# Sampled attention: masks laid into the score buffer, one operation that adds and takes the maximum, and two side products in other places

## What is computed

```python
def sel_attend(q, idx, q_pos, blocks, slopes):
    ...
    kv = blocks[b_ix, g_ix, idx]
    s = jnp.einsum('btgrd,bngjd->btgrnj', q, kv[..., 0, :])
    k_pos = idx[..., None] * SEL_BLOCK + jnp.arange(SEL_BLOCK, dtype=jnp.int32)
    dist = q_pos[None, :, None, None, None] - k_pos
    s = s - slopes[None, None, :, :, None, None] * dist[:, :, :, None].astype(jnp.float32)
    ...
    p = jax.nn.softmax(s.reshape(s.shape[:4] + (-1,)), axis=-1).reshape(s.shape)
    ...
    return jnp.einsum('btgrnj,btgnjd->btgrd', p, kv[..., 1, :])
```

## Time and profile before

| | |
|---|---|
| time, median of 3 runs | 2636.42 µs (2633.18 to 2641.44) |
| profiled execution: its time, its span | 2633.0 µs, 2630.7 µs |
| TensorE products busy | 2474.3 µs, 94% of the span |
| TensorE weight loads busy | 1994.0 µs, 76% |
| VectorE busy | 794.6 µs, 30% |
| ScalarE busy | 525.1 µs, 20% |
| GpSimd busy | 97.0 µs, 4% |
| mean granted TensorE clock | 0.957 of full speed |
| chain that ended last | PE 87%, DVE 7%, DMA 2%, ACT 2%, issue 1% |

### The profile page before, as it was taken

How to read it: one execution, slowest core, us unless ns; L and a number is a source line. 1 busy time by engine, 2 the same in 40 slices (tenths; PEclk the granted TensorE clock), 3 DMA queues, 4 the chain that set the end, 5 groups by cost and what they waited for, 6 DMA issues and landing times.

```text
span 2630.7 us, 31111 instructions
## 1 busy us (share of the span) xinstructions
PE 2474.3 (94%) x13222; PEld 1994.0 (76%) x13222; DVE 794.6 (30%) x1829; ACT 525.1 (20%) x1067; POOL 97.0 (4%) x182
## 2 busy tenths in 40 slices
PE   7999789999998999999999987999999989999998
PEld 5787567678887888888877865766788878888886
DVE  2444333642412112210015543356431122112001
ACT  1254111550101111110012531135310011111100
POOL 3010000000000000000000100000000000000000
PEclk8998899997999999999999978999989999999999
DMA  6444421111221222222262534211112212221222
GB/s 194 126 170 176 186 71 49 33 33 35 64 83 48 64 80 64 81 57 67 73 209 91 202 144 177 65 49 25 27 48 80 67 48 80 64 81 59 64 72 67
DMA packets 184576, 228.52 MB, mean 87 GB/s; under 512 B 37470, under 2 KB 170932, under 8 KB 180084
## 3 DMA queue, kind: packets, MB, share of 16 engines
q1 hardware_dynamic: 174008, 133.11, 17.2%
q0 software_dynamic: 10432, 93.44, 9.4%
HBM read 218.19 MB, written 16.66 MB: 89 GB/s over the span
## 4 chain that ended last, share of the span: by engine, by line
PE 87%; DVE 7%; DMA 2%; ACT 2%; issue 1%; DVEq 0%; SPq 0%; POOLq 0%; ACTq 0%
PE PS L790 50%; PE PS L1336 12%; PE PS L812 5%; PE PS L909 4%; DVE arena L1650 3%; PE PS L897 2%; ACT arena L1367 2%; PE PS L1141 1%; DMA arena<-in_cache_kv_slc_dram,idx 1%; PE PS L1152 1%; PE PS L1057 1%; PE PS L433 1%; DVE arena L1641 1%; PE PS L1254 1%; DMA arena<-in_state_kv_win_dram 1%
## 5 line engine op out<-in xcount | busy, mean ns | idle before, releaser
L790 PE MATMUL PS<-hT,ring 128*128 128x272 f32 x4608 | 1081.0, 397 | 14.0 <-DVE hT L1647 10.7
L790 PEld LDWEIGHTS PS<-hT,ring 128*128 128x128 f32 x4608 | 882.4, 192 | 208.6 <-issue 25.9
L1367 ACT ACTIVATE arena<-PS 64x512 f32<-64x512 f32 (+10 forms) x480 | 241.9, 525 | 1295.3 <-PE PS L790 709.7
L1336 PE MATMUL PS<-arena,ring 128*128 128x272 f32 x1408 | 323.5, 393 | 1.9 <-DVEq L2225 1.9
L1336 PEld LDWEIGHTS PS<-arena,ring 128*128 128x128 f32 x1408 | 267.2, 190 | 57.6 <-DVEq L2225 2.7
L1650 DVE COPY arena<-PS 64x512 f32<-64x512 f32 (+6 forms) x215 | 155.8, 726 | 323.3 <-PE PS L790 103.1
L1641 DVE TENSOR_TENSOR arena<-PS,arena 128x544 f32<-128x544 f32 (+3 forms) x120 | 73.1, 621 | 418.9 <-PE PS L790 399.5
L790 PE MATMUL PS<-arena,ring 128*128 128x272 f32 x768 | 177.2, 393 | 3.1 <-DVE arena L1641 3.1
L1647 DVE SCALAR_TENSOR_TENSOR arena<-arena,prm 128x32 f32<-128x32 f32 (+1 forms) x176 | 87.9, 500 | 291.2 <-ACT arena L1367 288.1
L790 PEld LDWEIGHTS PS<-arena,ring 128*128 128x128 f32 x768 | 145.8, 190 | 33.9 <-DVE arena L1641 4.0
L1641 DVE TENSOR_TENSOR xT<-PS,xT 128x544 f32<-128x544 f32 x32 | 23.2, 724 | 427.0 <-PE PS L1336 319.1
(11 more groups left out here) (278 smaller groups left out, 1644.9 us busy)
## 6 DMA issues: line engine op xcount, KB each, us to landing
ring<-in_w_up_dram SPq DMA_DIRECT2D x88, 512.0 KB, 4.6
ring<-in_w_in_dram SPq DMA_DIRECT2D x68, 512.0 KB, 4.7
ring<-in_w_down_dram SPq DMA_DIRECT2D x32, 384.0 KB, 3.8
ring<-in_w_down_dram SPq DMA_DIRECT2D x32, 320.0 KB, 4.4
arena<-in_state_kv_win_dram POOLq DMA_DIRECT2D x4, 2048.0 KB, 15.7
ring<-in_w_out_dram SPq DMA_DIRECT2D x16, 512.0 KB, 4.5
out_dram<-in_state_kv_win_dram POOLq DMA_DIRECT2D x2, 4064.0 KB, 22.7
ring<-in_w_in_dram SPq DMA_DIRECT2D x16, 256.0 KB, 4.8
```

The source lines that it names most:

```text
L790: mm = pe.matmul(PS[0:m, b + a, 0:HALF], weight(k), rhs(k)[:, HALF * a:HALF * a + HALF], start=(k == 0), stop=(k == nk - 1))
L1336: mm = pe.matmul(PS[:, b + a, 0:HALF], w[:, k, :], aT[:, 11 * half + k, HALF * a:HALF * a + HALF], start=(half == 0 and k == 0), stop=(hal ...
L1367: return nc.scalar.activation(out, in_, func, **kw)
```

## The change

Four things change.

1. The masks are laid into `z` before the scores come. Behind `window_values(hf)`, VectorE adds the chosen blocks' mask and the distances over all 2048 columns, copies the new tokens' scores and takes their maximum. When the scores of two quarters are there, one operation (`tensor_tensor_reduce`) adds them to what lies in `z` and takes the maximum of the sum. The window does likewise with `dwin`. The maxima of the parts are joined by small operations.
2. The window's steps of the first half are split: `window_probabilities(0)` (the transposes) comes ahead of the importance product, and `window_values(0)` behind the transposes of the compressed probabilities. A buffer `ptnw` of its own takes the window's new-token probabilities.
3. The side products move: `qb0` from behind the first window's scores to behind the compressed branch's output product, ahead of `turn_k(0)`; `kb1` from behind the second half's gathered scores to behind `window_values(1)`, ahead of `turn_k(0)` of that half. The places ("s", hf, 2) are new there, and ("s", 1, 0) is empty.
4. The value product of the gathered keys waits for the probabilities' two copies one by one, the first ahead of block 0, the second ahead of block 8, and for `ptn` at the end.

The diff, cut to its core:

```diff
-at = dict(zip((("s", 0, 2), ("s", 0, 0), ("s", 1, 1), ("s", 1, 0)), SIDE))
+at = dict(zip((("s", 0, 2), ("s", 0, 0), ("s", 1, 1), ("s", 1, 2)), SIDE))
...
-def window_values(hf):
...
-    xw = XB[xslot(f"win{hf}")[0]].rearrange("p l c -> p (l c)").rearrange("p (b r c) -> p b r c", b=4, r=4)
...
+def window_probabilities(hf):
...
+def window_values(hf):
...
+    xw = XB[xslot(f"win{hf}")[0]].rearrange("p l c -> p (l c)").rearrange("p (b r c) -> p b r c", b=4, r=4)
...
         bb = 32 * b4
-        mm = pe.matmul(PS[bb:bb + 32, b, 0:P], ptn[0:NS, bb:bb + 32], kv[0:NS, 4, 2, P:2 * P], start=False, stop=True)
+        mm = pe.matmul(PS[bb:bb + 32, b, 0:P], ptnw[0:NS, bb:bb + 32], kv[0:NS, 4, 2, P:2 * P], start=False, stop=True)
     mm.then_inc(*S.fill(pe, f"ow{hf}"))
...
 window_scores(0)
-side(("s", 0, 2))
+window_probabilities(0)
 pe.wait_ge(*S.at(pe, "pc_s", 1))
...
 mm.then_inc(*S.fill(pe, "pcT"))
+window_values(0)
 pe.wait_ge(*S.drained(pe, "pcT"))
...
         window_scores(hf)
-    window_values(hf)
+        window_probabilities(hf)
+        window_values(hf)
+    side(("s", hf, 2))
...
     b = S.banks(pe, f"os{hf}")
-    pe.wait_ge(*S.drained(pe, f"pt{hf}0"))
-    pe.wait_ge(*S.drained(pe, f"pt{hf}1"))
-    pe.wait_ge(*S.drained(pe, f"ptn{hf}"))
     for i in range(STRIDE):
+        if i % 8 == 0:
+            pe.wait_ge(*S.drained(pe, f"pt{hf}{i // 8}"))
         for b4 in range(4):
...
                       start=(i == 0), stop=False)
+    pe.wait_ge(*S.drained(pe, f"ptn{hf}"))
     for b4 in range(4):
...
+dv.wait_ge(*S.drained(dv, "sn"))
...
+    copy(zw[:, 512:512 + NS], snew[:, 2 + hf, :])
+    rmax(small[:, 100:101], snew[:, 2 + hf, :])
...
-    tt(zw[:, 0:512], PS[:, b, :], dwin[:, :], ALU.add).then_inc(*S.drain(dv, f"sw{hf}"))
+    nc.vector.tensor_tensor_reduce(zw[:, 0:512], PS[:, b, :], dwin[:, :], 1.0, -3e38, ALU.add, ALU.max, small[:, 99:100]).then_inc(*S.drain(dv, f"sw{hf}"))
...
-    copy(zw[:, 512:512 + NS], snew[:, 2 + hf, :]).then_inc(*S.inc(dv, "dve_step"))
-    dv.wait_ge(*S.last(dv, "dve_step"))
-    rmax(small[:, 23:24], zw).then_inc(*S.inc(dv, "dve_step"))
-    dv.wait_ge(*S.last(dv, "dve_step"))
-    tsc(small[:, 34:35], small[:, 23:24], nslope_c, ALU.mult).then_inc(*S.inc(dv, "nb_s"))
+    tsc(small[:, 34:35], small[:, 99:100], small[:, 100:101], ALU.max, nslope_c, ALU.mult).then_inc(*S.inc(dv, "nb_s"))
...
-side_copy(("s", 0, 2))
...
     dv.wait_ge(*S.last(dv, "dve_step"))
+    z4 = z[:, 0:2048].rearrange("p (l s f) -> p l s f", l=STRIDE, f=4)
+    tt(z4, bc(selml[:, :, :].unsqueeze(3), [P, STRIDE, NSEL - 1, 4]),
+       bc(dslc[:, :].rearrange("p (s f) -> p s f", f=4).unsqueeze(1), [P, STRIDE, NSEL - 1, 4]), ALU.add).then_inc(*S.inc(dv, "dve_step"))
+    copy(z[:, 2048:2048 + NS], snew[:, hf, :])
+    rmax(small[:, 98:99], snew[:, hf, :]).then_inc(*S.inc(dv, "dve_step"))
+    side_copy(("s", hf, 2))
+    dv.wait_ge(*S.last(dv, "dve_step"))
     turned_keys(dv, copy, hf, 0, 1)
...
-        tt(z[:, 1024 * lg:1024 * lg + 1024].rearrange("p (m n) -> p m n", m=8), PS[:, b:b + 2, :].rearrange("p a (m n) -> p (a m) n", m=4),
-           bc(dslc[:, :].unsqueeze(1), [P, 8, P]), ALU.add).then_inc(*S.drain(dv, f"ss{hf}{lg}"))
-    dv.wait_ge(*S.drained(dv, f"ss{hf}0"))
-    dv.wait_ge(*S.drained(dv, f"ss{hf}1"))
-    copy(z[:, 2048:2048 + NS], snew[:, hf, :])
-    z4 = z[:, 0:2048].rearrange("p (l s f) -> p l s f", l=STRIDE, f=4)
-    tt(z4, z4, bc(selml[:, :, :].unsqueeze(3), [P, STRIDE, NSEL - 1, 4]), ALU.add).then_inc(*S.inc(dv, "dve_step"))
-    dv.wait_ge(*S.last(dv, "dve_step"))
-    rmax(small[:, 22:23], z[:, :]).then_inc(*S.inc(dv, "dve_step"))
-    dv.wait_ge(*S.last(dv, "dve_step"))
-    tsc(small[:, 32:33], small[:, 22:23], nslope_c, ALU.mult).then_inc(*S.inc(dv, "nb_s"))
+        zl = z[:, 1024 * lg:1024 * lg + 1024]
+        nc.vector.tensor_tensor_reduce(zl, PS[:, b:b + 2, :].rearrange("p a n -> p (a n)"), zl, 1.0, -3e38, ALU.add, ALU.max,
+                                       small[:, 96 + lg:97 + lg]).then_inc(*S.drain(dv, f"ss{hf}{lg}"))
+        dv.wait_ge(*S.drained(dv, f"ss{hf}{lg}"))
+        if lg == 0:
+            tt(small[:, 98:99], small[:, 98:99], small[:, 96:97], ALU.max).then_inc(*S.inc(dv, "dve_step"))
+            dv.wait_ge(*S.last(dv, "dve_step"))
+    tsc(small[:, 32:33], small[:, 97:98], small[:, 98:99], ALU.max, nslope_c, ALU.mult).then_inc(*S.inc(dv, "nb_s"))
```

7 lines of the change are left out of this document (4 added, 3 removed).

## The result

| | before | changed |
|---|---|---|
| median, range of the runs | 2638.39 µs (2633.18 to 2641.44, 4 runs) | 2596.56 µs (2592.55 to 2599.19, 4 runs) |
| profiled execution: time, span | 2633.0, 2630.7 µs | 2598.69, 2596.8 µs |
| mean granted TensorE clock | 0.957 | 0.963 |

The changed kernel takes 0.9842 of the time before, 95% interval 0.9819 to 0.9865: 41.8 µs less. The forecast was 2607, in a range of 2598 to 2620. The direction held, but the median lies 1.4 µs under the range, and the gain is half again as large as the 27.8 µs forecast. A second set of four runs had its median at 2598.60, just inside the range.

What follows compares the result with a forecast made beforehand. TensorE was taken as busy nearly throughout, losing time only to waits and low clock. Per layer 7.8 + 1.1 + 1.8 + 1.0 + 4.7 = 16.4, less 2.5, is 13.9, 27.8 for two: 2607 µs, range 2598 to 2620.

Steps and rivals of the forecast that it cites:

- first half, up to the scores: Samples' first half: gather issued earlier, side product covers its wait, gathered scores begin at 270.6 instead of 278.43; 7.8 µs per layer.
- first half, after the scores: Behind the first half's gathered scores: side product stays, shorter VectorE path removes the 1.14 µs wait; 1.1 µs per layer.
- first value product: First half's value product of gathered keys: waits only for its first eight blocks at its start; 0.9 µs per layer.
- second half, up to the scores: Second half: side product fills the gathers' waits, but full DMA engines limit the gain; 1.0 µs per layer.
- second half, after the scores: Behind the second half's last scores: uncovered wait of 3.9 µs, ending at 349.8 instead of 354.55; 4.7 µs per layer won.
- second value product and the clock: Second half: 0.9 µs won by the value product's split wait, 2.5 lost to low clock behind the new wait, per layer.
- the side product, begun at the low clock, takes 8.8: First half, side product ahead of turning the gathered keys: starts at low clock, takes 8.8 µs as before, ends at 266.4.
- second rival: First half: clock rises earlier, small operations win back 1.6 µs, side product 1.2, capped at some 2 per layer; 2603, chance 0.12.
- 1.0 won, nothing if the weight load ... delays the last slice: Second half's gathers: 1.0 µs per layer won, none if the side product's released weight load delays the last slice a µs.
- I take 2.5: Behind the second half's new wait: low clock costs 2.5 µs per layer, between bounds of nothing and 7.8.
- first rival: Behind the new wait the clock stays low to the next side product: 7.8 instead of 2.5 µs per layer; 2618, chance 0.14.
- fourth rival: Slower: low clock holds far into the prompt's part, costing 29.2 µs per layer; 2659, chance 0.03.

Runs made afterwards that it cites:

- window_steps_late: The changed kernel with the first half's window transposes and values back behind the compressed branch's output product; 2608.15 µs, ratio 0.9879.
- kb1_old_place: The changed kernel with side product `kb1` back behind the second half's gathered scores; 2604.12 µs, ratio 0.9871.
- before_waits_filled: The kernel before with dummy transposes of the constant identity in TensorE's uncovered waits in the sampled stretch; 2631.44 µs, ratio 0.9973.

## Why the prediction was right in kind and too low in size

Per layer, in the traces of the forecast's kernel and of the changed one, µs won:

| term | forecast | layer 0 | layer 1 |
|---|---|---|---|
| first half, up to the scores | 7.8 | 9.00 | 9.95 |
| first half, after the scores | 1.1 | 1.36 | 1.59 |
| first value product | 0.9 | 1.12 | 1.12 |
| second half, up to the scores | 1.0 | −0.45 | 0.45 |
| second half, after the scores | 4.7 | 4.74 | 4.75 |
| second value product and the clock | 0.9 − 2.5 | −1.83 | −0.20 |
| sum | 13.9 | 13.9 | 17.7 |

The sum of layer 0 meets the forecast to the tenth by luck: the first half won 1.7 more than forecast, the second half's way to its scores 1.5 less, and the last row 0.2 less. The 3.8 above the forecast lie in layer 1.

**What held.** Each step that was to show is in the trace: no wait for a slice in the first half and 0.80 in the second of layer 0; the fourth gather of the first half issued 8.3 after the window's scores end; the combined operation at 1.2; one wait of 3.90 where 3.9 was forecast; the clock at 0.56 behind it. The transposes of the window start 4.02 after its scores began (forecast 4.05), and the side product 6.34 after that (forecast 6.5).

**First failed step: "the side product, begun at the low clock, takes 8.8".** It took 7.70 in layer 0 and 7.60 in layer 1. With the split, TensorE works through the small operations without a gap (6.14 of 7 µs busy at 0.50), and the clock is back as the product starts. In layer 1 it came back earlier still, and the small operations took 5.36 instead of 6.5 as well. window_steps_late, which has the waits again, gives the 8.89 of the forecast. So the second rival, given 0.12, came true for about half of its 2 µs in layer 0 (and in full in the second trace of the changed kernel, 21.4 instead of 22.4) and all of it in layer 1. The sum had counted the gap-free run as three waits removed and nothing more; what it does to the clock stood only in that rival.

**Second: "1.0 won, nothing if the weight load ... delays the last slice".** In layer 0 0.45 were lost. The side product took 9.66, not 8.8 or 9.05, but that is not what decided: a shorter one would only have made the 0.80 behind it longer. The last slice did. By the trace's DMA records the window and the four slices, 10 MB on GpSimd's queue, took 29.2 µs (291.6 to 320.8), where they had taken 28.1 (305.3 to 333.4); and from the wait's end to the scores it took 3.1 instead of the 2.7 counted. The forecast had said that an earlier issue doesn't help here, and that held; it had no room for a later landing except by the weight load, which began at 319.9, 0.9 before the end, and so can't be all of it. Over the fourteen traces the 10 MB take 27.0 to 29.3 µs, and what makes the difference is not shown. In layer 1 no slice was waited for, and half of the gain came. kb1_old_place prices the second half's move at between 1.3 and 5.5 µs for two layers.

**Third, the clock's cost.** "I take 2.5" per layer. The filled wait shows 1.2 in each layer up to the end of the samples' part, and 1.7 more in layer 0 in a product that is often as slow without the new wait. The 2.5 was counted in full for layer 1, too, where the earlier trace rows already had that product at 9.05; there it went to 9.29, and the last row of the table is −0.20, not −1.6. The Trainium skill ("TensorE: Matmul & The Clock Gate", section "Why this matters for your kernels") advises against idle gaps between bursts of matmuls, and the traces agree: behind the 3.90 the low clock comes, and the same kernel with the gap filled doesn't have it there. The first rival's 7.8 stayed far off: in the two traces of the changed kernel the transposes took 2.98 to 3.56 and the value product 3.70 to 4.19, not twice their 1.97 and 3.70.

**Fourth: the base.** The sum was made against one execution's stretches, 252.0, the shortest of three (mean 253.7), which hides 1.7 µs, nearly all in the prompt's first product. Of the 5.7 µs by which 33.5 exceeds the 27.8 of the forecast, 3.8 are in its own trace (252.0 − 220.4 = 31.6), and the rest is the draw of that one execution and of the changed one.

Two slips in the arithmetic change nothing: the terms given for the path after the last scores add up to 1.58, not 1.65 (the start of VectorE, 0.07 behind TensorE, is missing; 1.64 was measured), and the fourth rival's 2636 + 2 × 12.8 is 2662, not 2659.

**What stays open.** The medians differ by 40 to 42 µs, and 33.5 is what the stretches show. In the profiled executions the rest of the span adds 3.1 (2379.5 against 2376.4). But the six other kernels that carry all or most of the change spent 2377.6 to 2382.4 there, as the kernel before does, so this looks like the draw of single executions and not like an effect. The remaining 3 to 5 µs I can't place: two of the three profiled executions of before lie 3 to 5 below its median of about 2638, and whether the changed kernel's untouched stages gain anything was not settled.

## What to carry to other kernels

When a transfer is waited for, move independent dense work into the wait and shorten the path that this work used to cover in the same change: either alone leaves or exposes the other's wait, and here gave 9.0 or 7.5 µs, where both, with the order of the small steps and the single waits (5.4 and 6.5 when taken out), gave 33.5. When small operations are put in one unbroken run, price what follows them at the clock that such a run brings about, not at that of the old trace. Take the base from several executions with their granted clocks, and end the stretch that you compare with the work that the change touches. A wait that nothing useful fits can be filled with transposes of a constant: in five places per layer it won another 6 to 8 µs here, in the longest alone nothing that the median showed.

## What the runs showed of the hardware

- Transposes of a constant identity count as work for the clock. 5, 8 and 28 of them in waits of 1.4, 2.1 and 3.9 µs took the low clock in the two stretches from 46 to 8 µs.
- The time of one and the same kernel goes with its mean granted clock. Over the 51 executions of the kernel before that ran beside the experiments it was 2641 to 2643 µs at 0.953, 2637 to 2640 at 0.955, 2634 to 2637 at 0.957 and 2627 at 0.961. That is 1.8 µs for 0.001, with a correlation of −0.94. What makes the clock fall at other places from one execution to the next the records don't tell.
- A faster clock ahead of a transfer that is waited for is worth little: 45 µs less of the low clock gave 2.7 µs in the stretches of before_waits_filled, and 6.0 in its median.
- The second half's window and four slices, 10 MB on GpSimd's queue, took 27.0 to 29.3 µs in the two layers of all fourteen traces, whether TensorE waited or worked meanwhile.
- The combined addition and maximum costs what the addition costs: 0.69 for 512 columns, 1.21 to 1.23 for 1024 (the addition alone 1.21 to 1.23 in the kernel before), and 0.08 for the accumulator.
